# Late lower halves on GpSimd, columns on two engines, and a query projection of the unnormed input

## The reference

```
x = x + g1 * (mix @ w_out)
h = rmsnorm(x, g) * (1 + scale) + shift
q = h @ w_q                                  # 8 heads x 2 halves x 128
s, i = top_k(q . keys, 16)                   # per half, 128 keys
idx, gate = top 16 of the 256 pair sums, softmax
act = gelu(h . u[idx])                       # 16384 experts, 1024 wide
x = x + g2 * sum(gate * act * v[idx])
```

## Time and profile before

| | us |
|---|---|
| median of 3 runs | 4033.29 (4032.61 to 4034.79) |
| the profiled execution | 4038.78, span 4036.7 |
| TensorE busy | 3886.0 (96%) |
| VectorE busy | 3005.2 (74%) |
| ScalarE busy | 2336.3 (58%) |
| GpSimd busy | 1065.0 (26%) |
| granted TensorE clock, mean | 0.981 |

### The profile page before, as it was taken

How to read it: one execution, slowest core, us unless ns; L and a number is a source line. 1 busy time by engine, 2 the same in 40 slices (tenths; PEclk the granted TensorE clock), 3 DMA queues, 4 the chain that set the end, 5 groups by cost and what they waited for, 6 DMA issues and landing times.

```text
span 4036.7 us, 77215 instructions
## 1 busy us (share of the span) xinstructions
PE 3886.0 (96%) x27086; PEld 3431.7 (85%) x27086; DVE 3005.2 (74%) x5529; ACT 2336.3 (58%) x4301; POOL 1065.0 (26%) x670
## 2 busy tenths in 40 slices
PE   6999999999999999999998999999998999999999
PEld 6898888888889888888888988888887798888887
DVE  6758889777565888986766687987775568797555
ACT  4246579455533657954556566974454456696554
POOL 0104467000010445810000244741000024482000
PEclk9999999999999999999998999999998999999999
DMA  8335553878514555377853555458883255535654
GB/s 284 130 133 187 187 167 126 281 251 286 167 50 136 169 185 178 122 270 243 288 176 105 177 187 188 138 193 291 284 286 111 79 167 185 190 126 162 192 192 156
DMA packets 203685, 749.44 MB, mean 186 GB/s; under 512 B 22704, under 2 KB 23856, under 8 KB 202192
## 3 DMA queue, kind: packets, MB, share of 16 engines
q1 hardware_dynamic: 178416, 646.51, 48.2%
q0 software_dynamic: 25056, 100.15, 7.9%
HBM read 745.52 MB, written 1.05 MB: 185 GB/s over the span
## 4 chain that ended last, share of the span: by engine, by line
PE 77%; DVE 14%; issue 4%; ACT 3%; POOL 1%; DMA 1%; SPq 0%; DVEq 0%; ACTq 0%
PE ps L2084 16%; PE ps L2526 11%; PE ps L2533 11%; PE ps L2529 11%; PE ps L2092 9%; DVE t_lo L1205 4%; DVE arena L1908 4%; PE ps L2056 4%; PE ps L2057 3%; PE ps L2063 3%; PE ps L2233 2%; POOL t_lo L625 1%; DVE oh L1893 1%; ACT t_hi L717 1%; DVE arena L1900 1%
## 5 line engine op out<-in xcount | busy, mean ns | idle before, releaser
L717 ACT CAST t_hi<-raw 128x1024 fp32r<-128x1024 f32 x1180 | 1242.1, 1053 | 961.2 <-PE ps L2533 690.5
L1205 DVE TENSOR_TENSOR t_lo<-raw,t_hi 128x1024 fp32r<-128x1024 f32 x1004 | 1227.8, 1223 | 648.3 <-ACT t_hi L717 627.2
L2084 PE MATMUL ps<-h_both,t_hi 128*128 128x512 f32 x3040 | 762.2, 393 | 0.0
L625 POOL TENSOR_TENSOR t_lo<-raw,t_hi 128x1024 fp32r<-128x1024 f32 x176 | 450.6, 2560 | 734.1 <-ACT t_hi L717 734.1
L2084 PEld LDWEIGHTS ps<-h_both,t_hi 128*128 128x128 f32 x3040 | 546.6, 189 | 97.8
L2056 PE MATMUL ps<-h_both,t_hi 128*128 128x256 f32 x2304 | 602.4, 297 | 26.1 <-DVE h_both L1337 14.5
L2057 PE MATMUL ps<-h_both,t_hi 128*128 128x256 f32 x2304 | 579.4, 287 | 0.0
L2526 PE MATMUL ps<-t_hi,h_both 128*128 128x512 f32 x2048 | 548.0, 389 | 5.4 <-DVE h_both L1944 5.4
L2533 PE MATMUL ps<-t_lo,h_both 128*128 128x512 f32 x2048 | 547.5, 389 | 1.0 <-DVE t_lo L1205 1.0
L2529 PE MATMUL ps<-t_hi,h_both 128*128 128x512 f32 x2048 | 547.4, 389 | 0.0
L2056 PEld LDWEIGHTS ps<-h_both,t_hi 128*128 128x128 f32 x2304 | 450.7, 196 | 38.9 <-issue 29.5
(11 more groups left out here) (308 smaller groups left out, 4439.6 us busy)
## 6 DMA issues: line engine op xcount, KB each, us to landing
raw<-u_tiles SPq DMA_DIRECT2D x512, 512.0 KB, 3.4
raw<-v_tiles SPq DMA_DIRECT2D x512, 512.0 KB, 4.2
raw<-w_tiles SPq DMA_DIRECT2D x188, 512.0 KB, 3.8
oh<-w_tiles POOLq DMA_DIRECT2D x160, 512.0 KB, 4.8
arena<-w_tiles SPq DMA_DIRECT2D x16, 512.0 KB, 4.2
arena<-keys_t POOLq DMA_DIRECT2D x4, 1024.0 KB, 5.1
arena<-mla_w POOLq DMA_DIRECT2D x1, 4096.0 KB, 15.2
arena<-lora POOLq DMA_DIRECT2D x2, 1280.0 KB, 9.2
```

The costliest lines, as they stand in the source:

```text
L625: pool.tensor_tensor(t_lo[:, j % SPL, :], raw[:, j % RAW, :], t_hi[:, j % SPL, :].bitcast(F32), ALU.subtract).then_inc(lo_by_pool, 1)
L717: act.copy(t_hi[:, j % SPL, :], raw[:, j % RAW, :]).then_inc(hi_done, 1)
L1205: tts(t_lo[:, j % SPL, :], raw[:, j % RAW, :], t_hi[:, j % SPL, :].bitcast(F32), ALU.subtract).then_inc(lo_done, 1)
L2084: mm(ps[:, j % 2, :], hi[:, c, :], h_both[:, c, :, :].rearrange("p a t -> p (a t)"), start=(c == 0), stop=False)
```

## The change

Late stage:
- GpSimd no longer makes columns. `late_lowers` makes the lower halves of the u tiles 97 to 127, counting `lo_done` itself after VectorE's last one.
- VectorE makes 4 columns (`ACT_FROM = 4`) instead of 2, and no lower half. ScalarE makes 4, as before.
- `hot_rows` has two buffers, and `rows(m+1)` stands behind `columns(m+1)` instead of behind the wait for the gate products.

Query projection: the weights multiply gain * x, split into `g_hi` and `g_lo` (with two more columns that hold the shift), which ScalarE and VectorE make chunk by chunk beside the output projection. The product has 258 columns; the last two are the query projection of the shift. When rinv is known, VectorE copies that column to `q_bias`, multiplies the PSUM tile by rinv in place, and ScalarE adds the bias on the way out. The sums of squares stand behind the first query tile on TensorE and the spread of rinv in the second. `h_hi` and `h_lo`, which expert-up needs, are made one chunk a tile beside the query tiles 0 to 8. `keep_clock` is no longer called there.

```diff
-POOL_FROM, POOL_TO = 2, 4
+ACT_FROM = 4
...
-        hot_rows = acc[:, 0:512].bitcast(F16).rearrange("p (q k) -> p q k", q=8)
+        hot_rows = acc[:, :].bitcast(F16).rearrange("p (b q k) -> p b q k", b=2, q=8)
...
-            def middle_hots(l):
+            def late_lowers(l):
                 pool.wait_ge(sel_ready, TT * (l + 1))
                 pool.memset(act_slot(LATE, None), 1.0)
...
-                    for q in range(POOL_FROM, POOL_TO):
-                        t = 8 * m + q
-                        ins = pool.tensor_scalar(hot_cols[m % 2][:, q, :], iota, sel[:, 1, t:t + 1], sel[:, 2, t:t + 1],
-                                                 ALU.is_equal, ALU.mult)
-                    ins.then_inc(pooled, 1)
+                first = SEGS[f"u{l}"][0]
+                pool.wait_ge(lo_done, first + LATE + 2)
+                for j in range(first + LATE + 2, first + KEYS):
+                    pool.wait_ge(hi_done, j + 1)
+                    pool.tensor_tensor(t_lo[:, j % SPL, :], raw[:, j % RAW, :], t_hi[:, j % SPL, :].bitcast(F32),
+                                       ALU.subtract).then_inc(lo_done, 1)
...
             def uppers_and_squares(name, then):
+                def gained_and_square(c):
+                    act.wait_ge(taken, TAKEN[name] + c + 1)
+                    if c == 0:
+                        act.activation(g_hi[:, :, T:T + 2], mods[:, 24:32].unsqueeze(2).broadcast_to([P, DC, 2]), ACT.Identity)
+                    act.activation(g_hi[:, c, 0:T], x[:, c, :], ACT.Identity, scale=gain[:, c:c + 1]).then_inc(g_up, 1)
+                    square_of(c)
...
+            def queries(l):                       # ScalarE
+                for k in range(count):
+                    n, b = first + k, (first + k) % 2
+                    if k + 2 < count:
+                        upper(n + 2, n + 2, None, name)
+                    if k == 0:
+                        norm()
+                    seen(q_scaled)
+                    act.activation(tk["q"][:, k, :], ps[:, b, 0:T], ACT.Identity, bias=q_bias[:, k:k + 1]).then_inc(taken, 1)
+                    if k < DC:
+                        seen(normed)
+                        act.activation(h_hi[:, k, :], wide[:, k, :], ACT.Identity, bias=mods[:, 24 + k:25 + k]).then_inc(h_up, 1)
+                    if k + 2 >= count:
+                        upper(n + 2, n + 2, None, f"u{l}")
...
             def add_products(name, gate, g, then):
+                def gained_lower(c):
+                    seen(g_up)
+                    stt(g_lo[:, c, 0:T], x[:, c, :], gain[:, c:c + 1], g_hi[:, c, 0:T].bitcast(F32), ALU.mult,
+                        ALU.subtract).then_inc(g_split, 1)
...
+            def queries(l):                       # VectorE
+                for k in range(count):
+                    n, b = first + k, (first + k) % 2
+                    if k == 0:
+                        lower(n + 2, n + 2, name)
+                        inverse_root()
+                        seen(rinv_wide)
+                        link(cp(q_rinv, rinv_all))
+                    dve.wait_ge(tile_used, n + 1)
+                    cp(q_bias[:, k:k + 1], ps[:, b, T:T + 1])
+                    tts(ps[:, b, 0:T], ps[:, b, 0:T], q_rinv, ALU.mult).then_inc(q_scaled, 1)
+                    if k and k + 2 < count:
+                        lower(n + 2, n + 2, name)
+                    if k < DC:
+                        scaled_by(wide, gain, k, normed)
+                    if 1 <= k <= DC:
+                        lower_of(k - 1)
...
                 for k in range(LATE, KEYS - 1):
                     m = k - LATE
                     if m + 1 < GROUPS:
                         columns(m + 1)
-                    if k + 2 < KEYS:
-                        lower(first + k + 2, first + k + 2, name)
-                    else:
+                        rows(m + 1)
+                    if k + 2 == KEYS:
+                        dve.wait_ge(lo_done, first + KEYS)
                         lower(SEGS[f"v{l}"][0], SEGS[f"v{l}"][0], f"v{l}")
                     activated(k)
-                    dve.wait_ge(gates_t, GROUPS * l + m + 1)
-                    if m + 1 < GROUPS:
-                        rows(m + 1)
                     gate(m)
...
+            def queries(l, out_name):             # TensorE
+                for k in range(count):
+                    n = j = first + k
+                    pe.wait_ge(hi_done if k else lo_done, n + 1)
+                    pe.wait_ge(taken, k + (TAKEN[name] - 1))
+                    o = ps[:, j % 2, 0:T + 2]
...
+                    if k:
+                        if k == 1:
+                            spread_rows()
+                        pe.wait_ge(lo_done, n + 1)
...
+                    if k == 0:
+                        squares_of_out(out_name)
...
-                squares_of_out(name)
-                keep_clock(1, 7)
-                spread_rows()
-                keep_clock(3, 7)
-                peer(l)
+                peer(l, name)
```

More of the change, by code:

```diff
@@ L153 @@
 GROUPS = T // 8
+TQ = T + 4
+GAINED_AT = 18176
 LRU_BANKS = [2, 4, 6, 2]
@@ L246, in sem @@
             return ctx.enter_context(nc.semaphore(name))
+        with nc.sbuf_tensor("below_gained", [P, GAINED_AT], F32), \
+                nc.sbuf_tensor("gained", [P, 2, DC, TQ], F32R) as gained:
+            pass
         arena = sb("arena", [P, KEYS * T])
@@ L730, in uppers_and_squares @@
                     if k >= 3:
-                        act.wait_ge(taken, TAKEN[name] + k - 2)
-                        square_of(k - 3)
+                        gained_and_square(k - 3)
                 upper(first + count, first + count, None, then)
                 for c in range(count - 3, count):
-                    act.wait_ge(taken, TAKEN[name] + c + 1)
-                    square_of(c)
+                    gained_and_square(c)
+                upper(first + count + 1, first + count + 1, None, then)
             def project(name, take_out, then=None):
@@ L1067, in modulate_for @@
                     modulate(mods[:, 0:8])
[L1068 to L1071, removed]
                 else:
@@ L1088, in distances @@
                     act.wait_ge(gates_t, GROUPS * l + m - 1)
-                for q in range(4):
-                    t = 8 * m + 4 + q
-                    ins = act.activation(hot_cols[m % 2][:, 4 + q, :], iota, ACT.Abs, bias=sel[:, 1, t:t + 1], scale=-1.0)
+                for q in range(ACT_FROM, 8):
+                    t = 8 * m + q
+                    ins = act.activation(hot_cols[m % 2][:, q, :], iota, ACT.Abs, bias=sel[:, 1, t:t + 1], scale=-1.0)
                 ins.then_inc(away_done, 1)
@@ L1096, in weights @@
                 act.wait_ge(away_done, GROUPS * l + m + 1)
[L1097 to L1100, removed]
+                for q in range(ACT_FROM, 8):
+                    t = 8 * m + q
+                    ins = act.activation(hot_cols[m % 2][:, q, :], hot_cols[m % 2][:, q, :], ACT.Relu,
+                                         bias=sel[:, 2, t:t + 1], scale=minus_w[:, 4 * m + q - 4:4 * m + q - 3])
                 ins.then_inc(weighted, 1)
@@ L1242, in add_products, with lower_of @@
                         lower(first + count, first + count, then)
+                        gained_lower(k - 1)
                         link(add_square(4))
                         add_square(5).then_inc(squares_added, 1)
-                dve.wait_ge(taken, TAKEN[name] + count)
+                gained_lower(count - 2)
+                gained_lower(count - 1)
+                lower(first + count + 1, first + count + 1, then)
+            def queries(l):
+                name = f"q{l}"
+                first, count = SEGS[name][:2]
+                def lower_of(c):
+                    seen(h_up)
+                    stt(h_lo[:, c, :], wide[:, c, :], mods[:, 24 + c:25 + c], h_hi[:, c, :].bitcast(F32), ALU.add,
+                        ALU.subtract).then_inc(h_split, 1)
+                for k in range(count):
[14 more added lines that the diff above has]
+                        lower_of(k - 1)
             def add_bias(l, groups, bank):
@@ L1345, in modulated, with norm @@
                 lower_of(DC - 1)
-            def norm(g, scale, shift, then, begun=False):
+            def norm(g, scale, shift, then):
                 first = SEGS[then][0]
@@ L1352, in norm @@
                     modulation(3, [0, 1], 5, IN_NORM[3])
-                elif not begun:
+                else:
                     lower(first, first, then)
@@ L1890, in columns @@
                         dve.wait_ge(gates_t, GROUPS * l + m - 1)
-                    for q in range(POOL_FROM):
+                    for q in range(ACT_FROM):
                         t = 8 * m + q
@@ L2503, in gate @@
                         pe.wait_ge(gated, GROUPS * l + m - 1)
-                    for made, qs in ((hot, range(POOL_FROM)), (pooled, range(POOL_FROM, POOL_TO)),
-                                     (weighted, range(POOL_TO, 8))):
```

(1 more changed line is left out.)

59 lines of the change are left out of this document (40 added, 19 removed).

## The result

| | us |
|---|---|
| median after, 4 runs | 4088.57 (4086.18 to 4092.84) |
| median before, 4 runs beside them | 4034.04 (4032.61 to 4038.99) |
| after / before | 1.0131, 95% interval 1.0116 to 1.0145 |
| profiled execution after | 4086.18, span 4084.3 |

The change costs 54.5 us; 28 had been predicted. The direction was right, the size was not, and 4088.6 lies above the range's end of 4076. I account for the 47.6.

The account below looks back on a forecast made before the run. VectorE was taken to bound the late tiles at 4.34 us, with 7.4 us a layer lost at the hand-over. Late stage +40 and query projection -12 gave +28, 4061 us on the median; range 3990 to 4076.

Parts of the forecast that it names:

- the term for the late stage: Late expert-up tiles: 143.4 us instead of 133.5, so 9.9 us a layer added, 40 us in four.
- Exclusion of GpSimd and columns: Late stage: GpSimd's lower half and VectorE's columns exclude each other for the whole instruction; shared need 4.35 us a tile.
- GpSimd gets in between two operations of VectorE: Late stage: GpSimd can take its turn between two VectorE operations issued back to back; its lower half was put at 2.32 us.
- Rival B: Late stage: VectorE keeps the port from first column to rows, GpSimd always after; pace 4.35, total 4013 us; chance 17%.
- The loop of two tiles, 9.57 us: Late stage: upper half, GpSimd, columns and rows, gate and next products close a loop, 4.78 us a tile.
- Seven tiles at 4.10 before the loop closes: Late stage: GpSimd slips about 0.25 us a tile, so 7 tiles go at 4.10, then 24 at 4.78.
- VectorE alone 3.74 us: Late stage: VectorE's own work per tile, 4.34 less the 1.14 lower half plus two columns of 0.27.
- Hand-over: Output to query projection: third query tile at 8.6 us against 13.1; net gain 2.9 us a layer, 12 in four.
- Rival C: Query projection: ScalarE's order throttles all eight tiles, 8 x 0.6 eats the 4.5 gain; 4073 us; chance 8%.
- The clock at nothing: TensorE's granted clock without the dummy products at the hand-over: cost nothing; if it fell, 1.7 us a layer.

Follow-up runs that it names:

- late_only: The kernel before with the new late stage alone, without the new query projection: 4099.56 us, ratio 1.0150.
- iota_psum: The changed kernel with the index row that columns and rows compare with read from PSUM instead of SBUF: 3990.60 us, ratio 0.9874.
- vector_all: The changed kernel with all late lower halves back on VectorE, which keeps its four columns: 4109.79 us, ratio 1.0168.
- five_reordered: five_ordered with the row one-hots put between activated and gate instead of ahead of activated: 3979.88 us, ratio 0.9853.
- query_only: The kernel before with the new query projection alone, late stage as before: 4022.07 us, ratio 0.9952.
- ordered: The changed kernel with one more wait: GpSimd starts each late lower half only after VectorE has ended that tile's four columns: 4012.90 us, ratio 0.9929.
- no_lower: The changed kernel with GpSimd's late lower halves cut to 8 of 1024 columns, all waits kept: 4002.08 us, ratio 0.9899.
- rows_psum: The changed kernel with the index row read from PSUM for the row one-hots alone, columns still from SBUF: 4001.86 us, ratio 0.9900.
- five_ordered: The changed kernel with rows from PSUM, GpSimd's lower half after the columns, five columns on VectorE and three on ScalarE: 3997.66 us, ratio 0.9887.

## Why the prediction was wrong, point by point

The step that failed is the term for the late stage, +9.9 us a layer. It let the loop of two tiles close after seven tiles at 4.10 and put it at 9.57 us; the loop closed after five and measured 9.75, and the stage grew by 14.3 a layer. The second is the clock, put at nothing. The mechanism of the loss was the predicted one.

- **Exclusion of GpSimd and columns (the step that carried the sign): right.** The row of memsets had been the only one. After, the first of the columns takes 1.3 us in front of an unchanged rows operation (0.34 without GpSimd), and the three kernels that take the exclusion or GpSimd's time away all go at 4.09.
- **GpSimd gets in between two operations of VectorE: right.** At 1621.57 it did, before the fourth column. Rival B, GpSimd always behind the rows at a pace of 4.35, was possible but needs the order to be forced: with one wait it is real, at 4.25 and 4012.9 us.
- **The loop of two tiles, 9.57 us: the mechanism right, mis-sized.** Measured in the same terms: `upper` to GpSimd 1.12 (1.19), GpSimd 2.40 (2.32), columns' rest and rows 1.99 (2.03), signal to TensorE 0.15 (0.05), gate 0.89 (0.89), next tile's products and the signal to `upper` 3.20 (3.09): 9.75, 4.88 a tile and not 4.78. 0.1 on the 24 tiles of the forecast is 2.4 us a layer.
- **Seven tiles at 4.10 before the loop closes: wrong, five** (four in late_only). I let GpSimd slip by 0.25 a tile to the worst place. VectorE's columns slipped against GpSimd by 0.15, and the first time that GpSimd's issue fell before the last column, the order turned over at once. Two tiles at 0.78 more are 1.6 us. A third term was left out of the sum: the last of the 32 steps takes 3.7 instead of 3.3, 0.4 more. 9.9 + 2.4 + 1.6 + 0.4 = 14.3 a layer: over four layers 17 us, the greater part of the miss.
- **VectorE alone 3.74 us: too low by 0.16 to 0.17.** I had taken activated to gate as 0.33 from the earlier trace rows, where the rows follow activated. It did not decide the loop, but it made two of my expectations wrong (5.02 for 4.85, 4.13 for 3.97).
- **Hand-over: right, under-sized.** Third query tile after 8.20 us (8.6 predicted, though its terms add up to 8.5) against 13.13 to 13.56 before (13.1, which was the first layer's). From there to the scores 42.35 instead of 41.03: 1.3 lost, 1.6 predicted. Net 3.6 to 4.0 a layer, 15.4 in all, where 12 stood. Rival C, that ScalarE's order throttles every tile, is out: the tiles keep 2.88 to 2.94 but for two of 3.13, the ninth and the tenth, where the seventh or eighth was said. TensorE in the first layer, after:

```profile
240.51 0.28 PE L2554 MATMUL ps<-gained,t_hi 128*128 128x258 f32 x1
...
248.71 0.36 PE L2554 MATMUL ps<-gained,t_hi 128*128 128x258 f32 x1 [0.70 <-ACT arena L1143]
...
291.05 0.35 PE L2579 MATMUL ps<-arena 128*128 128x128 f32 x1 [1.19 <-ACT arena L1143]
```

- **The clock at nothing: wrong by place.** At the hand-over it was right (1.00 in 235 to 245 and in 245 to 250; before 0.83 in 235 to 245). But 30 us earlier, in code that the change does not touch, the first layer's 32 column sums ran at the lower level (granted 0.50 in 210 to 215), 6.8 us instead of 3.6. From the eight products in front of them to the end of the output projection it took 33.8 us instead of 29.2: 4.5 of the 5.9. The other 1.4 were there when the eight products started (206.75 against 205.34). That start varies in the traces without dummies, from 204.0 to 209.2.

Windows of the first layer, columns as in the earlier trace rows, after:

```profile
205.00:215.00 10.00, 9.44 (x50) 9.23 (x49) 6.42 (x15) 1.76 (x5) 0.00 (x0) 0.56 0.01 2
215.00:225.00 10.00, 10.00 (x66) 9.95 (x67) 3.27 (x6) 2.92 (x5) 0.00 (x0) 0.76 0.14 52
235.00:245.00 10.00, 10.00 (x84) 9.86 (x83) 8.16 (x15) 6.89 (x13) 0.00 (x0) 1.00 0.45 157
```

and iota_psum, as an execution in which it stayed up longer:

```profile
205.00:215.00 10.00, 9.49 (x70) 9.50 (x71) 5.64 (x15) 2.53 (x5) 0.00 (x0) 0.83 0.01 2
215.00:225.00 10.00, 9.80 (x81) 9.46 (x80) 6.73 (x10) 5.40 (x10) 0.00 (x0) 1.00 0.45 156
```

Before, late_only, vector_all, iota_psum and five_reordered show the second pattern and need 29.2 to 29.3 us for that stretch; query_only, ordered, after, no_lower, rows_psum and five_ordered show the first and need 33.6 to 34.0. iota_psum and rows_psum are the same program up to there, and kernels with the change's query part stand on both sides. So the 5.9 us are a difference of the two profiled executions and not shown to be a price of the change. What decides the level is open.

## What to carry to other kernels

When work is moved to an engine that shares a port with the one relieved, write the steady loop with the shared operations in the order in which they will be issued; here the order was worth 0.6 us a tile and the work moved 0.14, and one wait on the right moment turned a loss of 1.3% into a gain of 0.7% (the query part's gain, 0.5% by itself, is in both). Better is to take one side off the port: with a 128-column constant in PSUM for the rows the two engines hardly met. A pace read from starts holds only with the same neighbours; an operation that needs the result of the one just before it costs the difference.

## What the runs showed of the hardware

- GpSimd's lower half and a VectorE operation that contends with it run one after the other, each whole. Which is next when both wait is not told by their issue times: GpSimd, issued at 1621.57, went in front of a column issued 0.10 us later, but issued at 1617.48 it went behind the rows, issued 0.20 us later. In late_only GpSimd, issued at 579.20, ended before the column that had been issued at 579.15. What decides is open.
- A 128-column tensor_scalar with its source in PSUM is issued every 0.32 us, from SBUF every 0.26; a 1024-column tensor_tensor takes 1.21 from either.
- TensorE's granted clock can stand at 1.00 or at half of it (1.2 GHz) for the same 32 one-column products, 3.6 or 6.8 us, in two kernels that are the same up to there.
